# Where the activations of a two-block network lie in SBUF: pads before h, the MLP's u, the mixers' y and the gate weights

## Time and profile before

| | |
|---|---|
| median of 3 runs | 961.68 us (961.62 to 961.88) |
| the profiled execution's span | 959.9 us; the launch's own time about it makes up the difference to the runs, some 1.8 us |
| PE matmul busy | 951.5 us, 99% |
| PE weight load busy | 804.0 us, 84% |
| DVE, ACT, POOL busy | 632.8, 558.8, 101.2 us |
| DMA | 152.87 MB, mean 159 GB/s |
| granted TensorE clock | 9 tenths or more in all slices |

### The profile page before, as it was taken

How to read it: one execution, slowest core, us unless ns; L and a number is a source line. 1 busy time by engine, 2 the same in 40 slices (tenths; PEclk the granted TensorE clock), 3 DMA queues, 4 the chain that set the end, 5 groups by cost and what they waited for, 6 DMA issues and landing times.

```text
span 959.9 us, 14235 instructions
## 1 busy us (share of the span) xinstructions
PE 951.5 (99%) x5648; PEld 804.0 (84%) x5648; DVE 632.8 (66%) x1148; ACT 558.8 (58%) x926; POOL 101.2 (11%) x146
## 2 busy tenths in 40 slices
PE   9999999999999999999999999999999999999997
PEld 7777888888888777788888888999988899988876
DVE  6767687763545565677775354866569657577875
ACT  6697555543435777564553342755586556377774
POOL 0210000000000000000000035344013000411101
PEclk9999999999999999999999999999999999999999
DMA  9833465555554333245555565234332734421201
GB/s 365 313 125 135 162 219 188 200 182 195 175 200 164 144 125 139 88 145 207 179 200 192 189 235 185 89 132 148 116 132 89 282 99 167 162 102 45 89 22 46
DMA packets 22418, 152.87 MB, mean 159 GB/s; under 512 B 2512, under 2 KB 2768, under 8 KB 4944
## 3 DMA queue, kind: packets, MB, share of 16 engines
q1 hardware_dynamic: 21424, 148.51, 43.4%
q0 software_dynamic: 640, 3.15, 1.0%
q10 hardware_dynamic: 288, 0.30, 0.1%
HBM read 150.90 MB, written 1.05 MB: 158 GB/s over the span
## 4 chain that ended last, share of the span: by engine, by line
PE 97%; DVE 1%; ACT 1%; issue 0%; ACTq 0%; DVEq 0%
PE bank L190 20%; PE bank L192 19%; PE bank L191 19%; PE bank L1166 12%; PE bank L1167 6%; PE bank L932 2%; PE bank L2310 1%; PE bank L2319 1%; PE bank L2334 1%; PE bank L956 1%; PE bank L762 1%; PE bank L1602 1%; PE bank L945 1%; PE bank L1587 1%; PE bank L1579 1%; DVE w_hi_lo L160 1%
## 5 line engine op out<-in xcount | busy, mean ns | idle before, releaser
L160 DVE TENSOR_TENSOR w_hi_lo<-raw,w_hi_lo 128x2048 fp32r<-128x2048 f32 x121 | 277.5, 2296 | 134.8 <-ACT w_hi_lo L156 134.6
L156 ACT ACTIVATE w_hi_lo<-raw 128x2048 fp32r<-128x2048 f32 x135 | 257.6, 1911 | 108.8 <-PE bank L192 108.3
L1166 PE MATMUL bank<-h,w_hi_lo 128*128 128x512 f32 x512 | 181.2, 396 | 0.0
L1167 PE MATMUL bank<-h,w_hi_lo 128*128 128x256 f32 x512 | 144.4, 282 | 0.0
L190 PE MATMUL bank<-h,w_hi_lo 128*128 128x256 f32 x448 | 129.4, 289 | 0.1
L191 PE MATMUL bank<-h,w_hi_lo 128*128 128x256 f32 x448 | 125.1, 279 | 0.0
L192 PE MATMUL bank<-h,w_hi_lo 128*128 128x256 f32 x448 | 125.0, 279 | 0.0
L1166 PEld LDWEIGHTS bank<-h,w_hi_lo 128*128 128x128 f32 x512 | 96.2, 188 | 23.5 <-issue 0.2
L192 PE MATMUL bank<-w_hi_lo,mlp_u_lo 128*128 128x512 f32 x256 | 100.6, 393 | 0.0
L190 PE MATMUL bank<-w_hi_lo,mlp_u_hi 128*128 128x512 f32 x256 | 100.3, 392 | 0.0
L191 PE MATMUL bank<-w_hi_lo,mlp_u_hi 128*128 128x512 f32 x256 | 99.8, 390 | 0.0
(11 more groups left out here) (403 smaller groups left out, 1620.6 us busy)
## 6 DMA issues: line engine op xcount, KB each, us to landing
raw<-in_chunks SPq DMA_DIRECT2D x136, 1024.0 KB, 4.8
even_bias<-in_even POOLq DMA_DIRECT2D x8, 384.0 KB, 3.4
xres<-in_x SPq DMA_DIRECT2D x2, 512.0 KB, 5.4
raw<-in_chunks SPq DMA_DIRECT2D x2, 512.0 KB, 6.5
ml_z<-in_ml SPq DMA_DIRECT2D x1, 896.0 KB, 5.8
small<-in_small SPq DMA_DIRECT2D x1, 559.5 KB, 12.1
final_gain<-in_fnorm SPq DMA_DIRECT2D x1, 512.0 KB, 4.2
out<-final_xn SPq DMA_DIRECT2D x1, 512.0 KB, 2.6
```

The lines of the kernel that those rows point to most:

```text
L156: act.activation(w_hi[slot][:, :], raw[slot][:, :], ACT.Copy).then_inc(hi_ready, 1)
L160: dve.tensor_tensor(w_lo[slot][:, :], raw[slot][:, :], w_hi[slot][:, :].bitcast(F32), ALU.subtract).then_inc(lo_ready, 1)
L1166: pe.matmul(dst[:, :], w_hi[slot][:, cols], h[:, k, :, :], start=(k == 0), stop=False)
L1167: last = pe.matmul(dst[:, 0:S], w_lo[slot][:, cols], h[:, k, 0, :], start=False, stop=(k == KT - 1))
```

## The change

Pads of float32 columns are declared ahead of some tensors, so that all that follow in the same stack move up. No pad is read or written. One tensor is declared with another row length. No instruction is added, removed or moved, and no wait.

```diff
     const = sb(ctx, "const", [P, const_n])
+    sb(ctx, "pad_h", [P, 16])
...
     mlo_at = sb(big, "mlo_stats", [P, 5, TT])
+    sb(big, "pad_stage", [P, 32])
...
     bias = [sb(es, f"even_bias{i}", [P, 2, 3 * P]) for i in range(N_BIAS)]
+    sb(es, "pad_even_y", [P, 48])
     ey_hi = sb(es, "even_y_hi", [P, KT, S], F32R)
...
     oqg = sb(os_, "odd_qg", [P, 1])
+    sb(os_, "pad_odd_y", [P, 56])
     wf_hi = sb(os_, "wf_hi", [P, KT * HEADS], F32R)
...
             self.mv = sb(stack, "ml_mv", [P, ML_HEADS, TT, 2])
+            sb(stack, "pad_ml_y", [P, 40])
             with ExitStack() as tmp:
...
             self.y_hi = sb(stack, "ml_y_hi", [P, ML_TILES, S], F32R)
-            self.y_lo = sb(stack, "ml_y_lo", [P, ML_TILES, KW], F32R)[:, :, KW - S:KW]
+            self.y_lo = sb(stack, "ml_y_lo", [P, ML_TILES, S], F32R)
...
                 self.rt = [sb(tmp, f"nsa_rt{i}", [P, 2, S]) for i in range(2)]
+                sb(tmp, "pad_wg", [P, 48])
                 self.wg_hi = sb(tmp, "nsa_wg_hi", [P, KT * GW], F32R)
```

## The result

The changed kernel takes 964.33 us (median of 9 runs, 964.07 to 964.72), the kernel before 961.68 us (9 runs beside it, 961.48 to 962.21): ratio 1.0027, 95% interval 1.0017 to 1.0036. It is 2.65 us slower. The profiled span grew by 2.5 us, from 959.9 to 962.4.

What follows compares the result with a forecast made beforehand. TensorE's matmul spacings were taken to bound the kernel. Favourable terms of 17.8 us, less 0.8, made -17 us on the profiled 959.9: 942.9, plus 1.8 between span and runs gave 944.7 us; range 941 to 962.

Steps and rivals of the forecast that it cites:

- What bounds the kernel: Whole kernel: TensorE busy 951.5 of 959.9 us, waits 2.2 us, so an edit counts only by matmul spacing.
- That the distance modulo 256 sets the spacing: Split products: the same three 512-column matmuls take 682 or 700 ns by distance between ring and tensor; not proved by rows.
- the pairs: MLP up, 512 pairs of 512 and 256 columns: 352 to 341 ns each, saving 5.6 us; unfavourable 0.
- rival C: All products: place doesn't matter, spacings come from tile order and queue state; 961.7 us, chance 0.13.
- rival B: Place matters only where the ring streams; with h moving, how the stream was entered sets spacing; 955.5 us, chance 0.20.
- 128 is as good as the best spacing seen: All split products at distance 128: 682 ns for three 512-column matmuls, 340 for three of 256; savings sum to 17.8 us.
- MLP down: MLP down projection, 256 products: 688 to 682 ns saves 1.5 us; 688 to 700 costs 3.1.
- the unfavourable end: All split products: 128 as bad as the worst row of its width, 700 and 354 ns; sum +4.8 us.
- h stationary: 512-column products with h as stationary tile, 168 of them: 700 to 682 ns saves 3.0 us; unfavourable 0.
- One level for both widths: 512 and 256 columns: 128 gives the good spacing at both, 682 and 340 ns, and pairs at 341.
- Rival D: All split products: 128 is the worst place, MLP down above 688, h stationary stays at 700; 966.5 us, chance 0.12.
- That savings reach the end: Whole kernel: all MLP savings reach the end; 0.8 us taken off for h products outside the MLPs.

Runs made afterwards that it cites:

- the run with u's low part: Kernel with h at distance 64 and the rest at 0, but u's low part alone at 32: 959.25 us, ratio 0.9975 against the kernel before.
- mixture: Changed kernel with each tensor at another distance (h 64, u and NSA's y 32, even y 96, odd y 160, mLSTM y 192): 962.56 us, ratio 1.0009.
- h by stage: All y and u at 0, h placed per stage (inputs 0, MLP up 32, mLSTM and NSA 192): 952.01 us, ratio 0.9899 against the kernel before.

## Why the prediction was wrong

**What bounds the kernel: right.** The time went with the spacings and with nothing else. PE's waits stayed at 2.3 us, and the experiments' kernels, from 952.0 to 965.6 us, issue the same work.

**That the distance modulo 256 sets the spacing: right, and shown for 512 columns; for the pairs and for 256 columns it is not the only thing.** Between the four rivals I could only argue it. Exchanging the distances exchanges the levels of u and h (mixture); shifting by 256, or moving ring and tensors together, leaves them. So rival C falls. That one place can have two levels comes on top, and is taken up with rival B below. The Trainium skill's statement in "TensorE: Matmul & The Clock Gate", section "Step-by-step: what each phase is for", that the next tile's load takes no bandwidth from the running matmul, had been taken to mean that the place can't matter. That conclusion is not borne out: 680 and 703 ns for the same three matmuls at distances 0 and 160. Whether the load itself is what collides, the run with u's low part leaves open, so the statement on the ports is not refuted by itself.

**The step that failed: "128 is as good as the best spacing seen".** It was the favourable end of a range whose two ends I had at 682 and 700, and I took it because 128 resembles 0 against halves of 256 and because the mLSTM's low y showed no peak there. The runs put 128 at 697.1 ns for 512 columns, near the bad end. The mLSTM rows could not carry the argument: their high part stood at 224, and there the low part's place says little. Over all of its products, those with the low tile at 0 average 693.5 ns and those at 128 695.1, 1.6 ns apart, while with both parts at one place 0 gives 680.3 and 128 gives 697.1. Term by term: MLP down +2.6 us where -1.5 was forecast (the unfavourable end was +3.1); h stationary -0.7 for -3.0; odd, mLSTM, even and NSA outputs together +0.5 for -1.7. The last two are small because most of these products stood near 700 before and stand near 697 now.

**One level for both widths: wrong.** I carried the resemblance over to 256 columns and to the pairs. Each width has its own order of places: 0 is the best for 512 (680) and nearly the worst for 256 (359.4); 32 is bad for 512 (700.0) and, with 160, the best for the pairs (346.7). With h moving at 128 the 256 columns cost +1.2 us for -6.0 forecast, the pairs gave -1.1 for -5.6. Even all at 0, the place that earned 680, brought only 4.2 us.

**Rival B's mechanism, half right.** Some places have two levels. With 256 columns at distance 64 or 192 they are 340 and 353; a stretch shows its level from the first or second product and keeps it up to the next break. A shift by 256 bytes flipped one such stretch. With pairs at distance 0 they are 346.7 in MLP 0 and 353.3 in MLP 1, which is as much as lies between the best and the worst place of the pairs. At 512 columns no two levels 13 ns apart were seen, only smaller steps at a break: 680.0 and 685.1 with u at 16, 693.3 and 696.7 with u's low part at 32. So B is right in that some stretches carry a rhythm on, and wrong in that place does not count with h moving: all stretches at 0 and at 96 stand at 360, all at 224 at 355, and 340 was seen at 64 and 192 alone. What decides which level a stretch takes is not shown. The 340 at distance 64 was thus no sign that any place could reach it.

**Rival D: the one whose number came nearest,** 964.3 for its 966.5. It had its place (MLP down first) and point (MLP down above 688, h stationary at 700, measured 698) right. Its price was 2 us high: the pairs gained 1.1, h stationary 0.7, and MLP down and the outputs lost less than at the worst row, while h moving lost 0.9 more. Its claim that 128 is the worst place is wrong: at 697.1 ns it is better than 32, 96, 160, 192 and 224, and no run shows the mechanism that it named. I gave it 0.12, and drew the range's upper end at 962 to leave it out. With two ends of a cost as far apart as these and no row for the new place, the two should have had nearly the same chance.

**That savings reach the end: right.** With h by stage the sum by levels gave 951.5 and 952.0 was measured; for h at 64 it gave 954.4 and 955.5 came.

## What to carry to other kernels

Where PE is full, read the spacing from start to start, not the duration, and compare it between places that do the same matmul with other tensors. Whether the streamed and the stationary tile stand well to each other is a matter of their distance modulo 256 and of the width, to a few bytes, and at some places of the rhythm that the stretch fell into; it has to be measured for each width, since the order of places is not one that a rule of thumb (0, or half the period) gives. One kernel that puts each tensor at another distance measures many places in one run, and the levels add up to within about 1 us in the two kernels where the sum was made beforehand from measured levels (954.4 for 955.5, 951.5 for 952.0). A mean over a whole kernel can hide two levels: look at the stretches one by one.

## What the runs showed of the hardware

- Three float32r matmuls of 512 columns take 680 to 703 ns by the distance of the two tiles alone. Three of 256 columns take 340 to 360 and a pair of 512 and 256 columns 347 to 353, by distance and, at some distances, by which of two levels the stretch has. The worst is 2 to 6% above the best, with the clock granted whole (2.4 GHz) and with DVE (632.7 to 633.3 us) and ACT (558.6 to 559.1) as busy as before.
- The dependence fits a period of 256 bytes (one shift by 256 left all means of 512 columns, of the pairs and of 256 columns with h moving) and is sharp: 0 gives 680, 8 gives 700, 16 gives 680 to 685, 252 gives 697.
- At one and the same place a stretch can run at either of two levels: 340 or 353 ns (256 columns, distances 64 and 192), 356 or 360 (256 columns, 128), 346.7 or 353.3 (pairs, 0).
- No mean came under 680 ns for 3 x 512 columns. That is 6% above 640 ns, an estimate that counts one cycle of 2.4 GHz for a column and that no run reaches. What that rest is, stays open, as does what exactly collides and why the widths differ.
